# Transposes between the last sums of each norm, low-weight products between them, and four other reorderings in a three-layer transformer kernel

## The reference, cut to what matters

```python
# block 1: differential attention + causal pooling, cross-attention to 256 memory rows, swiglu
h = rmsnorm(x, g);  proj = h @ w_in                  # q, k, v, u
da = diff_attention(rope(q), rope(k), v, lam)        # 4 heads, 2 maps each
po = einsum(causal_multiscale_pool(u), w_pool) * pool_scale
x += rmsnorm(concat(da, po) @ w_out, g);  x += rmsnorm(cross_attention(x) @ w_xo, g)
x += rmsnorm((silu(hf @ w_gate) * (hf @ w_up)) @ w_down, g)
# block 2: retention (4 heads, group norm, silu gate) + sparse attention (8 heads:
#          compressed, selected and window branches), swiglu
o_r = (o_r - mean) * rsqrt(var + 1e-5) * silu(rg);  x += concat(o_r, o_n) @ w_out
# block 3: HGRN2 (8 heads, chunked recurrence), swiglu, final RMS norm
o = o * rsqrt(mean(o*o)) * norm_g * sigmoid(gp);  x += o @ w_out
return rmsnorm(x, final_g)
```

## Time and profile before

| | |
|---|---|
| median of 3 runs | 1060.56 us (1060.43 to 1061.0) |
| the profiled execution: its own time | 1061.05 us |
| its span, first to last instruction | 1058.3 us |
| TensorE busy | 1035.2 us |
| VectorE busy | 736.0 us |
| ScalarE busy | 517.6 us |
| mean granted TensorE clock | 0.997 |
| load of a weight unit, issue to landing (median) | 4.8 us |
| high part of a unit on ScalarE, low part on VectorE | 1.90 us, 2.28 us |

### The profile page before, as it was taken

One profiled execution on the slowest core, in us unless ns is written; L12 is line 12 of the kernel. 1 busy time (PEld: TensorE's weight loads), 2 busy tenths in 40 slices (PEclk: granted clock), 3 DMA queues, 4 the chain that ended last, 5 costly groups with the idle time before them and its releaser, 6 DMA issues.

```text
span 1058.3 us, 17065 instructions
## 1 busy us (share of the span) xinstructions
PE 1035.2 (98%) x6902; PEld 916.4 (87%) x6902; DVE 736.0 (70%) x938; ACT 517.6 (49%) x669; POOL 31.7 (3%) x48
## 2 busy tenths in 40 slices
PE   8999999999999999999999999999999999999997
PEld 7988899788888879988788888888999888888885
DVE  6967575468878545888758778736689767778842
ACT  6866365454344435856454353435543354353531
POOL 1000000000000001000000000001000010000000
PEclk9999999999999999999999999999999999999999
DMA  9833554254554746434145555754544235555531
GB/s 346 333 117 120 199 185 154 80 179 161 199 195 163 270 164 259 163 124 155 45 155 179 195 182 179 258 192 151 195 148 138 92 144 183 194 179 184 194 139 40
DMA packets 27291, 183.38 MB, mean 173 GB/s; under 512 B 3201, under 2 KB 3473, under 8 KB 6113
## 3 DMA queue, kind: packets, MB, share of 16 engines
q1 hardware_dynamic: 25200, 175.27, 46.3%
q0 software_dynamic: 1744, 7.16, 1.9%
q10 hardware_dynamic: 288, 0.11, 0.0%
HBM read 181.48 MB, written 1.05 MB: 172 GB/s over the span
## 4 chain that ended last, share of the span: by engine, by line
PE 86%; DVE 6%; ACT 5%; issue 2%; POOL 0%; POOLq 0%; DVEq 0%; ACTq 0%
PE GT L1707 11%; PE D L1707 10%; PE GT L1669 8%; PE GT L1671 7%; PE GT L1670 7%; PE D L1670 7%; PE D L1671 7%; PE D L1669 7%; PE GT L1705 5%; PE D L1705 5%; ACT s_whi L449 2%; PE D L2346 1%; DVE s_wlo L916 1%; PE GT L1867 1%; PE GT L1711 1%
## 5 line engine op out<-in xcount | busy, mean ns | idle before, releaser
L916 DVE TENSOR_TENSOR s_wlo<-s_raw,s_whi 128x2048 fp32r<-128x2048 f32 x164 | 372.8, 2277 | 186.4 <-ACT s_whi L449 186.1
L449 ACT ACTIVATE s_whi<-s_raw 128x2048 fp32r<-128x2048 f32 x164 | 307.7, 1900 | 96.1 <-PE D L1671 72.1
L1707 PE MATMUL GT<-s_x,s_whi 128*128 128x512 f32 x528 | 162.1, 393 | 0.0
L1707 PE MATMUL D<-s_x,s_whi 128*128 128x512 f32 x480 | 146.9, 392 | 0.0
L1669 PE MATMUL GT<-s_x,s_whi 128*128 128x256 f32 x384 | 108.6, 283 | 1.5 <-DVE s_x L944 1.5
L1671 PE MATMUL GT<-s_x,s_wlo 128*128 128x256 f32 x384 | 107.2, 279 | 0.0
L1670 PE MATMUL GT<-s_x,s_whi 128*128 128x256 f32 x384 | 107.0, 279 | 0.0
L1669 PE MATMUL D<-s_whi,s_hTh 128*128 128x512 f32 x264 | 104.2, 395 | 0.0
L1670 PE MATMUL D<-s_wlo,s_hTh 128*128 128x512 f32 x264 | 104.2, 395 | 0.0
L1671 PE MATMUL D<-s_whi,s_hTl 128*128 128x512 f32 x264 | 104.2, 395 | 0.0
L1705 PEld LDWEIGHTS GT<-s_x,s_wlo 128*128 128x128 f32 x462 | 84.4, 188 | 16.9
(11 more groups left out here) (361 smaller groups left out, 1684.5 us busy)
## 6 DMA issues: line engine op xcount, KB each, us to landing
s_raw<-in_stream SPq DMA_DIRECT2D x164, 1024.0 KB, 4.8
s_gb<-in_rows POOLq DMA_DIRECT2D x4, 512.0 KB, 4.1
s_xn<-in_x SPq DMA_DIRECT2D x2, 512.0 KB, 4.4
s_raw<-in_stream SPq DMA_DIRECT2D x4, 256.0 KB, 6.6
s_y<-in_mem POOLq DMA_DIRECT2D x1, 1024.0 KB, 10.2
s_w<-in_cmpw POOLq DMA_DIRECT2D x1, 1024.0 KB, 10.0
out<-s_y SPq DMA_DIRECT2D x4, 256.0 KB, 2.0
s_poolm<-in_poolm POOLq DMA_DIRECT2D x1, 768.0 KB, 12.0
```

Source lines behind the costliest of these rows:

```text
L449: nc.scalar.activation(whi[:, u % RING, 0:n], raw[:, u % RING, 0:n], ACT.Copy)\
L916: nc.vector.tensor_tensor(wlo[:, u % RING, 0:n], raw[:, u % RING, 0:n], whi[:, u % RING, 0:n], ALU.subtract).then_inc(lo_ready, 1)
L1707: ins = nc.tensor.matmul(o[:, f, :], hi[:, kt, c[f]], x2[:, kt, :], start=kt == 0, stop=kt == KT - 1)
```

## The change

Nothing is computed differently, apart from the order of some sums and of two factors of the final norm.

1. Norm boundaries. At norms 5 to 7 chunk 2 is transposed inside the last sum unit (between the two halves of its last bank); at norms 3 and 4 it still follows `keep_clock`. Then: chunk 1, low-weight products of tiles 0 and 1, chunk 3, low-weight products of tiles 2 and 3, and the high-weight products tile by tile. `first_columns` accumulates in `DB[0]` instead of `G[0]`. Norm 2 keeps its old order under the names `first_queries` and four `chunk_transposes`.
2. Pooled products go to `TB[0]`, `TB[1]`; the wait for the memory tiles (`xT_ready`, 16) moves behind unit 7.
3. In the differential attention VectorE's first weight split moves behind the probabilities of the first two steps.
4. Sparse attention: the copies `npT_win(h + 1)` and, for even h, `npT_slc(h + 1)` move ahead of the weight split of step h; `ret_scores(0)` and `(1)` move between the transposes of heads 6 and 7.
5. Retention: the group norm runs in two halves of two heads (`ret_centred`, `ret_variance`, `ret_gated`, `ret_scaled`); its transposed result goes to tiles 4 to 7.
6. HGRN: `hg_transposes(0)` moves into the middle of unit 15; heads 0 to 3 get buffers `ah`, `al` of their own, so that `hg_hi(0)`, `(1)` run before unit 15 is evacuated.
7. Final norm: multiplication by the gain first (VectorE), by the root afterwards: chunks 0 to 2 on ScalarE, which also issues the store of chunk 2; chunk 3 on VectorE.

```diff
@@ ScalarE, sparse attention, HGRN, end
             pcT_half(1)
+            npT_slc(0)
             split(u0 + 7 + RING)
             for p in range(4):
                 for h in (2 * p, 2 * p + 1):
-                    npT_slc(h)
...
+                    if h % 2 == 0:
+                        npT_slc(h + 1)
                     if h < 5:
                         split(u + RING)
                 n_hi(p)
+                if p < 3:
+                    npT_slc(2 * p + 2)
...
             for j in range(8):
...
+                if j == 7:
+                    hg_hi(0)
+                    hg_hi(1)
                 if j % 4 < 2:
                     evac_rows(u0 + 8 + j, vh[:, :, c], vh_scale)
...
+            for c in range(3):
+                act.wait_ge(sem("out_gained"), c + 1)
+                act.wait_ge(rstd_ready, pow_at(f"fin.{c // 2}") + 1)
+                nc.scalar.activation(chunk(y, c), chunk(y, c), ACT.Copy, scale=rstd[:, POW_COL[f"fin.{c // 2}"]])\
+                    .then_inc(sem("out_scaled"), 1)
@@ VectorE
             maxes(0)
             maxes(1)
-            split(kv0 + RING)
             probs(0)
             probs(1)
+            split(kv0 + RING)
...
+            npT_win(0)
+            split(u0 + 7 + RING)
+            for h in range(8):
+                if h < 6:
+                    n_max(2 * h + 4)
+                    n_max(2 * h + 5)
+                if h < 3:
+                    rope_turn(1 + h, qk[1 + h], braw, "_b")
+                if h < 6:
+                    n_probs(2 * h + 4)
+                    n_probs(2 * h + 5)
+                if h < 2:
+                    rope_cos(2 + h, u0 + 8 + h, qk[2 + h], "_b")
+                if h < 7:
+                    npT_win(h + 1)
+                if h < 5:
+                    split(u0 + 8 + h + RING)
+                if h % 2 and h < 6:
+                    n_lo(h // 2)
...
             ret_decay(3)
+            ret_centred(0)
             ret_copy(2)
             ret_copy(3)
...
+            ret_variance(0)
+            ret_centred(1)
+            ret_gated(0)
+            ret_scaled(0)
+            ret_variance(1)
+            ret_gated(1)
+            ret_scaled(1)
...
+            add_sum("dn2", "f1", out_gained)
+            out_gained(1)
+            norm_mean(8, "fin", 1)
+            out_gained(2)
+            out_gained(3)
+            dve.wait_ge(rstd_ready, pow_at("fin.1") + 1)
+            dve.wait_ge(sem("out_gained"), 4)
+            nc.vector.tensor_scalar(chunk(y, 3), chunk(y, 3), rstd[:, POW_COL["fin.1"]], None, ALU.mult)\
+                .then_inc(sem("last_scaled"), 1)
@@ TensorE
+            def block_low(u, o, n, kt, first):
+
+                lo = wlo[:, u % RING, :].rearrange("p (k n) -> p k n", k=KT)
+                pe.wait_ge(sem("norm_hi"), KT * n + kt + 1)
+                for f in range(2):
+                    nc.tensor.matmul(o(f), lo[:, kt, P * f:P * f + P], xTh[:, kt, :], start=kt == 0 and f <= first,
+                                     stop=False)
+
+            def boundary(n, u, o, first):
+
                 if n < 5:
                     chunk_transposes(n, 0)
...
                     keep_clock(norm_banks(n)[3], 2)
+                    chunk_transposes(n, 2)
+                chunk_transposes(n, 1)
+                wait_unit(u)
+                block_low(u, o, n, 0, first)
+                block_low(u, o, n, 1, first)
+                chunk_transposes(n, 3)
+                block_low(u, o, n, 2, first)
+                block_low(u, o, n, 3, first)
...
                     for kk in range(2):
+                        if n is not None and b == 3 and kk == 1:
+                            chunk_transposes(n, 2)
...
-            pe.wait_ge(sem("xT_ready"), 16)
...
-                o = halves(DB[g // 2][:])[:, g % 2, :]
+                o = halves(TB[g // 2][:])[:, g % 2, :]
...
             unit(u0 + 7, columns)
+            pe.wait_ge(sem("xT_ready"), 16)
...
+                    if h == 6:
+
+                        pe.wait_ge(sem("n_max"), 16)
+                        ret_scores(0)
+                        ret_scores(1)
...
-            unit(u0 + 15, rows)
-            hg_transposes(0)
+            unit(u0 + 15, rows, between=lambda: hg_transposes(0))
             level(7, 1)
```

More of the change, by code:

```diff
@@ L355, in _ @@
                 sp.dma_start(raw[:, u % RING, :], stream[u, :, :]).then_inc(landed[u % RING], 16)
-            for c in range(4):
-                sp.wait_ge(sem("out_ready"), c + 1)
+            for c, ready in ((0, "out_scaled"), (1, "out_scaled"), (3, "last_scaled")):
+                sp.wait_ge(sem(ready), c + 1 if c < 3 else 1)
                 sp.dma_start(out[c // 2 * P:c // 2 * P + P, 512 * (c % 2):512 * (c % 2) + 512], chunk(y, c))\
@@ L417, in _ @@
             pool.dma_start(cmps[:], cmps_in).then_inc(sem("cmps_in"), 16)
-            power("gn")
+            power("gn0")
+            power("gn1")
             power("f0.0")
@@ L892, in _ @@
             mlp(2)
-            norm_squares(8, xn, lambda c: chunk(y, c), 7)
+            norm_squares(8, xn, lambda c: (sg, hb)[c // 2][:, c % 2, :], 7)
+            for c in range(3):
[3 more added lines that the diff above has]
+                    .then_inc(sem("out_scaled"), 1)
+            act.wait_ge(sem("out_scaled"), 3)
+            act.dma_start(out[P:2 * P, 0:512], chunk(y, 2)).then_inc(sem("stored"), 16)
         @block.vector
@@ L1025, in post_norm, with add_sum @@
                 update(3)
-            def add_sum(ph, late=None):
+            def add_sum(ph, late=None, gained=None):
                 for c in range(4):
@@ L1037, in add_sum @@
                     ins.then_inc(sem("x_part"), 1)
-                    if ph == "dn2" and c == 1:
+                    if gained is not None and c == 1:
+                        dve.wait_ge(sem("x_part"), 4 * 6 + 1)
+                        gained(0)
                         norm_mean(8, "fin", 0)
@@ L1575, in hg_lo @@
                 dve.wait_ge(sem("hg_hi"), b + 1)
-                nc.vector.scalar_tensor_tensor(xTl[:, 2 * b:2 * b + 2, :], halves(DB[b][:]), gain("hgrn"),
-                                               xTh[:, 2 * b:2 * b + 2, :], ALU.mult, ALU.subtract)\
+                dst, high = (al, ah) if b < 2 else (xTl, xTh)
+                nc.vector.scalar_tensor_tensor(dst[:, 2 * b:2 * b + 2, :], halves(DB[b][:]), gain("hgrn"),
+                                               high[:, 2 * b:2 * b + 2, :], ALU.mult, ALU.subtract)\
                     .then_inc(sem("hg_lo"), 1)
@@ L1871, in first_columns, with half, first_queries @@
             def first_columns(u, n):
+                def half(f):
+                    return DB[0][:, S * f:S * f + S]
+                hi = whi[:, u % RING, :].rearrange("p (k n) -> p k n", k=KT)
+                boundary(n, u, half, 0)
+                for kt in range(KT):
+                    pe.wait_ge(sem("xT_ready"), KT * n + kt + 1)
+                    if kt >= 4:
+                        block_low(u, half, n, kt, 0)
+                    for f in range(2):
+                        c = slice(P * f, P * f + P)
+                        nc.tensor.matmul(half(f), hi[:, kt, c], xTh[:, kt, :], start=False, stop=False)
+                        ins = nc.tensor.matmul(half(f), hi[:, kt, c], xTl[:, kt, :], start=False,
+                                               stop=kt == KT - 1 and f == 1)
+                ins.then_inc(unit_done, 1)
+            def first_queries():
+                u, n = BASE["xq"], 2
                 hi, lo = (w[:, u % RING, :].rearrange("p (k n) -> p k n", k=KT) for w in (whi, wlo))
@@ L2077, in _ @@
             late_kv(6)
-            norm_transposes(2)
+            for c in (0, 2, 1, 3):
+                chunk_transposes(2, c)
             late_kv(7)
@@ L2392, in _ @@
             pe.wait_ge(sem("hg_lo"), 1)
-            sum_unit("oo", 0, between={1: lambda: level(8, 1), 2: lambda: hg_out(1)})
+            sum_unit("oo", 0, ah, al, 0, between={1: lambda: level(8, 1), 2: lambda: hg_out(1)})
             pe.wait_ge(sem("hg_lo"), 2)
-            sum_unit("oo", 1, between={2: lambda: hg_transposes(1)})
+            sum_unit("oo", 1, ah, al, 2, between={2: lambda: hg_transposes(1)})
             for j in range(2, 4):
```

157 lines of the change are left out of this document (70 added, 87 removed).

## The result

The changed kernel takes 1042.44 us in the median of 4 runs (1041.59 to 1042.93), the kernel before 1060.49 (1060.18 to 1061.0) beside it: ratio 0.9827, 95% interval 0.9812 to 0.9843. It is faster by 18.05 us, 1.7%. The profiled execution of after took 1042.93 us, its span is 1040.8.

What follows compares the result with a forecast made beforehand. The prediction took TensorE, busy 1035.2 of 1058.3 us, as the bound and priced its waits. Seven terms summed to 13.3 us, taking the median from 1060.56 to 1047.3 us, range 1045.0 to 1051.0.

Steps and rivals of the forecast that it cites:

- The diff keeps the products, so the second view is TensorE's waits: Whole kernel: products unchanged, so the gain was sought in TensorE's waits; busy time only about 1.6 us less.
- Part 2: Pooled products: the wait of 3.0 + 0.15 us goes, and 1.55 of low clock; 4.7 us, bounds 3.0 to 4.9.
- Part 3: Differential attention: TensorE's wait for probabilities behind VectorE's split goes; 0.8 us, bounds 0 to 0.9.
- The walk: Differential attention: next maxima start about when they did, and TensorE has another unit, 5.5 us, before needing them.
- Part 1: Five norm boundaries: stalls of 3.35 us go, less 0.65 and 0.2; 2.5 us, bounds 1.3 to 3.3.
- the 0.65 for eight changes from transposes to products: Norm boundaries: each added change makes the first product longer, eight x 0.08 = 0.65 us against the gain.
- Part 4: Sparse attention: `npT` copies ahead of splits remove waits of 2.95 us, less small delays; 2.7 us, bounds 1.5 to 3.6.
- Part 5: Retention: group norm in halves removes nearly all of the 1.5 + 0.15 us wait; 1.5 us, bounds 0.9 to 1.65.
- Part 6: HGRN: the wait for `hg_lo(0)` goes, 0.4 us for unit 15's evacuation comes; 0.8 us, bounds 0.4 to 1.3.
- Part 7: Kernel end: one scale on each of two engines replaces two VectorE operations; 0.3 us, bounds 0 to 0.95.
- The low clock: Rival, boundaries: the low clock is moved, not saved; one stretch costs 1.6 us, giving 1048.9; chance 0.09.
- The weight stream: Rival: delayed splits make six units each over 2.5 us late, 15 us, giving 1062; slower had chance 0.03.

## Why the prediction was right, and where it was wrong

- **The failed step** is "The diff keeps the products, so the second view is TensorE's waits". The products are the same, their price is not: `h_pad` stood in the diff (the list of changes above leaves it out) and got no price at all, neither 0 nor bounds. It is 4.34 of the 17.5 us, shown in both directions. All upper bounds together, 16.6, are less than the 17.5 that the span lost: no choice within them could have reached it. What remains is 13.1 us against 13.3 forecast; after without the pad took 1047.85, against 1047.3. That this agrees so well is in part luck: Parts 1, 4, 5 and 6 gave 1.5 more than forecast, Parts 3 and 7 gave 1.8 less.
- **Part 2** was right in both terms, 3.18 and 1.50 against 3.15 and 1.55, and shown by undoing it.
- **Part 3** was wrong by the mechanism named as its lower bound, "the wait comes back one step later". The walk looked at the next maxima; the next meeting of the two engines is at the copies of head 0, behind the split of the next unit, for which the transposes of head 1 wait (0.62, and 0.69 by starts). They had 0.3 us to spare before, and VectorE's list up to them is no shorter. One head later for the splits, and 0.82 us came out, about the 0.8 forecast.
- **Part 1** was mis-sized, 3.27 against 2.5. The 0.65 for eight changes from transposes to products is mostly not there: inside the sum, four transposes and the product behind them take 0.67 us from start to start (847.62 to 848.29), which is 4 x 0.11 + 0.23, and from 849.89 to the first high-weight product at 851.80 it is 1.91 for work that makes 1.82. The longer first product of the earlier trace rows overlaps the transposes. At norms 3 and 4 this stretch, from the first transposes behind the wait, takes 2.61 us each and 2.45 with the products last; whether these 0.16 are the change or the wait for high parts, which the prediction put at 0.1, was not separated. The cover of chunk 3 was as foreseen at norms 5 to 7.
- **Part 4**, 3.02 against 2.7: the stall that was to stay is there, 0.7 ahead of `n_out(3)`, and `n_scores` waits for nothing. The copies' place is shown for 1.1 of it only.
- **Part 5**, 1.66 against 1.5: nothing is left of the wait. The straight line's 1.03 for a power of 4 columns was right for the first half (1.04); the second took 1.42, with a VectorE operation beside it. **Part 6**, 1.05 against 0.8: the wait of 0.4 foreseen for unit 15's evacuation is the "issue" row in the waits. Its own terms, 1.15 - 0.4 + 0.2, make 0.95 and not 0.8; and 0.2 of the gain is an address again, in no term: 48 products of the output sum read `ah` and `al`, a multiple of 256 bytes from `whi`, and start every 229.3 ns, where with `x2` they took 233.3.
- **Part 7** had the wrong sign in the traces, -0.87 against 0.3, by something in no row of before: a load of instructions under the last store. With the load elsewhere the part gives 0.04, since the sum followed the last operations (0.7 earlier, more than forecast) and not the stores, which start no sooner. The root came at 1035.93, inside the second gain product (1034.84 + 1.29 = 1036.13) and 0.4 behind the end of the first, just as in before; the term of up to 0.55 for the second product was nothing. The rule of the Trainium skill, "SBUF — State Buffer", "SBUF: two separate sides", as the prediction read it, would have put it 0.4 us behind the second product; the trace does not agree, and the measurement decides.
- **The rivals.** The low clock did not move elsewhere in the profile of after; in some others it comes behind the 15-column products, where the same kernel has it in one execution and not in the next, and the kernel before with the pad alone has it too. The weight stream never became late.

## What to carry to other kernels

Price every line of a diff, the declarations too: a pad that nothing reads moved 792 products by 5.6 ns each and was a quarter of the gain. If TensorE's busy time falls by more than the waits and the clock explain, compare the mean of one product by form before looking for anything else. Where a wait is taken away by moving a long operation back in a queue, the queue is no shorter for it: find the next place where the other engine meets it, behind later operations that were not moved, and how much room there was. When the end of a kernel changes, look at the packets of its stores: when the last ones start, what shares the DMA engines with them.

## What the runs showed of the hardware

- Products of 128x512 start every 226.7 ns when their operands lie a multiple of 256 bytes apart in each partition, 229 with the stationary one 64 bytes ahead of such a place, and 233 to 234 at the six other places tried; with 256 columns a distance of 0 is the slowest of four (119.5 against 117.8 ns; in the kernel 120 against 115 with x stationary).
- An 8 KB load of instructions (309 ns) that meets a store delays its last packets by 0.74 us; moving it by twenty instructions in two queues took this away.
- A fall of the granted clock to 0.50 for 3.4 us, 1.5 us of time, starting 0.4 to 1.3 us behind the end of 32 products of 15 columns (1.96 us), in five of the thirteen profiles of the whole kernel.
- Powers on GpSimd: 0.55 us for one column, 1.04 for 4, 1.64 for 8 (at 503.73 and 830.50 in after); with a VectorE operation of two SBUF inputs beside them 0.93 for one and 1.42 for 4.
